# A new order for the softmax, state and transpose steps of a hybrid attention block

## The reference

```python
h = rmsnorm(x, norm_g); proj = h @ w_in
gk = jax.nn.log_sigmoid(gk_lr @ w_gk_up + b_gk) / 16
o_gla  = rmsnorm(gla_chunked(q, k, v, gk), gla_norm_g) * silu(gate_g)       # 4 heads, chunks of 64
o_pool = (multiscale_pool(u_p) @ pool_w) * pool_scale * silu(gate_p)
s = einsum('bthd,bmhd->bhtm', q_m, k_m) * 64 ** -0.5                        # 4 heads, 256 memory tokens
o_mem  = einsum('bhtm,bmhd->bthd', softmax(s), v_m) * silu(gate_m)
y = rmsnorm(x + concat(o_gla, o_pool, o_mem) @ w_out, final_g)
```

## Time and profile before

| | |
|---|---|
| Median of 3 runs | 1545.3 us (1544.16 to 1546.3) |
| The profiled execution: its time, its span | 1545.3 us, 1543.8 us |
| Mean granted TensorE clock | 0.973 |
| Busy share of TensorE, VectorE, ScalarE, GpSimd | 93%, 47%, 39%, 15% |
| One block of the loop | 87.8 us |

### The profile page before, as it was taken

How to read it: one execution, slowest core, us unless ns; L and a number is a source line. 1 busy time by engine, 2 the same in 40 slices (tenths; PEclk the granted TensorE clock), 3 DMA queues, 4 the chain that set the end, 5 groups by cost and what they waited for, 6 DMA issues and landing times.

```text
span 1543.8 us, 28261 instructions
## 1 busy us (share of the span) xinstructions
PE 1443.0 (93%) x11746; PEld 1046.2 (68%) x11746; DVE 724.0 (47%) x1221; ACT 608.1 (39%) x1101; POOL 236.4 (15%) x217
## 2 busy tenths in 40 slices
PE   3359699999999999999999999999999999999996
PEld 2238476776867677676867677686867767686762
DVE  2876625436172535527163544627163543616253
ACT  1344425344342534434252534434262534434241
POOL 1231201121110201121020202121020112112000
PEclk9669799999999999999999999999999999999998
DMA  8130100102010010102001010202001010201001
GB/s 337 65 136 1 42 2 28 54 0 82 0 69 12 27 54 10 71 0 82 0 36 46 27 54 0 82 0 82 0 27 54 21 61 0 82 0 46 10 28 68
DMA packets 15432, 69.32 MB, mean 45 GB/s; under 512 B 2352, under 2 KB 2480, under 8 KB 12848
## 3 DMA queue, kind: packets, MB, share of 16 engines
q1 hardware_dynamic: 15408, 68.98, 11.9%
HBM read 52.20 MB, written 16.78 MB: 45 GB/s over the span
## 4 chain that ended last, share of the span: by engine, by line
PE 90%; DVE 4%; ACT 2%; DMA 1%; issue 1%; POOL 1%; SPq 1%; DVEq 0%; ACTq 0%; POOLq 0%
PE bank L330 75%; PE bank L484 2%; PE bank L452 2%; PE bank L490 2%; PE bank L476 2%; PE bank L498 2%; DVE whl L852 1%; PE bank L541 1%; DVE wmx L816 1%; PE bank L463 1%; PE bank L388 1%; DMA whl<-in_pool_w 1%; PE bank L435 1%; PE bank L380 1%; POOL arena L1134 1%
## 5 line engine op out<-in xcount | busy, mean ns | idle before, releaser
L330 PE MATMUL bank<-arena,whl 128*128 128x256 f16 x6144 | 684.6, 274 | 2.6 <-DVE whl L852 2.6
L330 PEld LDWEIGHTS bank<-arena,whl 128*128 128x128 f16 x6144 | 602.3, 98 | 84.1 <-issue 6.5
L330 PE MATMUL bank<-arena 128*128 128x512 f16 x1536 | 344.1, 381 | 6.4 <-DVE arena L872 6.4
L330 PEld LDWEIGHTS bank<-arena 128*128 128x128 f16 x1536 | 147.8, 98 | 181.3 <-issue 15.4
L963 DVE SCALAR_TENSOR_TENSOR arena<-arena 64x256 f32<-64x256 f32 x60 | 25.2, 420 | 314.6 <-POOL arena L1191 313.2
L330 PE MATMUL bank<-whl,arena 128*128 128x512 f16 x768 | 168.3, 379 | 0.0
L686 ACT ACTIVATE arena<-bank,sca 128x512 f32<-128x512 f32 x64 | 43.9, 688 | 254.4 <-PE bank L330 253.3
L330 PEld LDWEIGHTS bank<-whl,arena 128*128 128x128 f16 x768 | 75.2, 99 | 86.9
L1143 POOL TENSOR_TENSOR arena<-arena 128x1024 f16<-128x1024 f32 x32 | 77.8, 2451 | 285.7 <-ACT arena L621 285.7
L1134 POOL TENSOR_TENSOR arena<-arena 128x1024 f32<-128x1024 f32 (+2 forms) x48 | 76.7, 1599 | 231.7 <-ACT arena L599 222.6
L1184 POOL TENSOR_TENSOR arena<-arena 128x542 f32<-128x542 f32 x16 | 17.4, 1090 | 606.1 <-ACT arena L693 598.3
(11 more groups left out here) (154 smaller groups left out, 1467.9 us busy)
## 6 DMA issues: line engine op xcount, KB each, us to landing
arena<-in_xt SPq DMA_DIRECT2D x16, 1024.0 KB, 5.2
arena<-in_x SPq DMA_DIRECT2D x32, 512.0 KB, 3.3
out<-arena SPq DMA_DIRECT2D x32, 512.0 KB, 2.6
arena<-in_w_in SPq DMA_DIRECT2D x8, 768.0 KB, 16.1
arena<-in_w_out SPq DMA_DIRECT2D x1, 4096.0 KB, 12.2
arena<-in_w_in SPq DMA_DIRECT2D x8, 392.0 KB, 16.2
arena<-in_w_mem SPq DMA_DIRECT2D x1, 2048.0 KB, 11.0
arena<-in_memt SPq DMA_DIRECT2D x1, 1024.0 KB, 6.6
```

The lines of the kernel that those rows point to most:

```text
L330: mm = nc.tensor.matmul(ap, lhs, rhs, start=k == 0 and n == 0, stop=(k, n) == last)
```

## The change

It changes the order of steps in the programs of TensorE, ScalarE and VectorE and nothing else. On TensorE the chunk states go ahead of scores 2 and 3, `quarter(1)` goes behind `turn_p(0, 6)`, and `turn_p(2, 6)` goes ahead of `quarter(2)` and the sum of squares. On ScalarE the table load goes ahead of `ket`, and `p_hi_of(3)` behind `norm_y`. On VectorE `p_norm(1)` goes ahead of `p_low(0)`, `state(0)` and `state(1)` go ahead of `mem_max(2)` and `(3)`, and `p_low(3)` goes behind `pt_copy(1, 7)`.

```diff
@@ TensorE @@
                 quarter(0)
+                states(0)
+                states(1).then_inc(pe_st, 1)
                 mem_scores(2)
                 mem_scores(3)
-                states(0)
-                states(1).then_inc(pe_st, 1)
-                quarter(1)
                 pe.wait_ge(sT_ok, 2 * i + 1)
                 turn_p(0, 6)
+                quarter(1)
                 pe.wait_ge(sT_ok, 2 * i + 2)
                 turn_p(1, 7)
+                pe.wait_ge(pt_out, 4 * i + 1)
+                turn_p(2, 6)
                 quarter(2)
                 if not last:
                     pe.wait_ge(p_exp, 4 * i + 4)
                     rms_sum(i + 1)
-                pe.wait_ge(pt_out, 4 * i + 1)
-                turn_p(2, 6)
                 pe.wait_ge(pt_out, 4 * i + 2)
                 turn_p(3, 7)
@@ ScalarE @@
                 silu(6, 3, 6)
+                nc.scalar.preload_act_table_set(EXP_LN)
                 act.wait_ge(pe_ket, i + 1)
...
                                      ACT.Copy).then_inc(ket_out, 1)
-                nc.scalar.preload_act_table_set(EXP_LN)
@@ ScalarE @@
                 p_hi_of(2)
-                p_hi_of(3)
                 if not first:
                     norm_y(i - 1, 0)
+                p_hi_of(3)
@@ VectorE @@
                 p_norm(0)
+                p_norm(1)
                 p_low(0)
-                p_norm(1)
                 p_low(1)
                 rows(0)
+                state(0)
+                state(1)
                 mem_max(2)
                 mem_max(3)
-                state(0)
-                state(1)
                 pt_copy(0, 6)
                 p_norm(2)
                 p_norm(3)
                 p_low(2)
-                p_low(3)
                 rows(1)
                 state(2)
                 pt_copy(1, 7)
+                p_low(3)
                 state(3)
                 pt_copy(2, 6)
```

## The result

The changed kernel takes 1582.7 us (median) against 1544.7 us before: 2.4% slower, ratio 1.0241 (95% interval 1.0221 to 1.0261), or 38.0 us. 1587.5 us were predicted, with a range of 1571 to 1607. Of the changed kernel's timed executions three took 1580.9 to 1582.8 us and one, in a slow state that no trace explains, 6496.0 us; the ratio leaves that one out.

What follows compares the result with a forecast made beforehand. TensorE, with no waits in loop blocks 1 to 14, was taken to bound the kernel. 14 x 2.70 = 37.8, plus 0.9, 0.2 and 3.3, made 42.2 us on 1545.3: 1587.5 us, range 1571 to 1607.

Steps and rivals of the forecast that it cites:

- What bounds it: Loop blocks 1 to 14: TensorE has no wait there, so a new order can only cost nothing or add waits.
- Edit 1: Table load ahead of ket on ScalarE: ket ends later, so TensorE's quarter(0) starts 0.85 us late in each block.
- The release: Time from ket's end to the start of the waiting quarter(0): taken as 0.1 us, bounds 0.05 to 0.15.
- Edit 2: States ahead of scores 2 and 3, reciprocals together, state(0) and (1) ahead of maxima: maxima 0.11 us later.
- Edit 3: turn_p(2) ahead of quarter(2), turn_p(0) ahead of quarter(1): TensorE waits another 1.85 us for p_low(2) in each loop block.
- the two waits: Waits for ket (0.85 us) and p_low(2) (1.85): 2.70 per loop block; a smaller first makes the second larger.
- Edit 4: p_hi(3) behind norm_y, p_low(3) behind pt_copy(1): turn_p(3) keeps 1.9 us of slack, so no cost.
- The ends: Block 15 0.9 us longer (bounds 0.85 and 2.70), block 0 about 0.2 us longer (bounds -1.7 and +1).
- Clock: TensorE's granted clock in the loop: two falls behind the new pauses, 3.3 us, between bounds of nothing and 23.4.
- B: Rival: the pauses make the clock fall in most blocks, 9 to 14 falls, 1599 to 1608 us; chance 0.25.
- Sum: Whole kernel: 37.8 us for the loop, plus 0.9, 0.2 and 3.3, is 42.2 us slower.

Runs made afterwards that it cites:

- undoing edit 1: The changed kernel with only the table load put back behind ket on ScalarE; 1581.2 us, ratio 1.0238.
- edit 4 undone: The changed kernel with p_hi(3) ahead of norm_y and p_low(3) behind p_low(2) again; 1581.3 us, ratio 1.0242.
- edit 3 alone: The kernel before with turn_p(0) moved ahead of quarter(1) and turn_p(2) ahead of quarter(2); 1579.3 us, ratio 1.0229.

## Why the prediction was right

- **What bounds it.** No wait in the loop before, so nothing to gain. All twelve variants agree: none is faster by more than can be measured, and each loss in the loop is a wait of TensorE, plus falls of its clock.
- **Edit 1, 0.85 us late**: measured 0.99. The release was mis-sized: the matmuls start 0.24 us behind ket's end (785.25 to 785.49), not 0.1, and outside the bounds of 0.05 to 0.15, which came from a release by VectorE. It has no effect on the sum, since the wait ahead of turn_p(2) shrinks by as much.
- **Edit 2, maxima 0.11 us later**: measured 0.07.
- **Edit 3, turn_p(2) bound to p_low(2), 2.70 us a block**: measured 2.67; the wait itself 1.51 of idle time. That the two waits share one end, and do not add, was the step that mattered, and undoing edit 1 showed it.
- **Edit 4 at nothing**, with quarter(2) as its cover: right for this kernel. The words "the cover is quarter(2)" were wrong as they stand: quarter(2) stands there in the kernel before too, and there edit 4 costs 0.75 us a block. What covers it is that the whole of TensorE is late, by 2.67 us in the changed kernel.
- **The ends.** Block 15's quarter(0) was 0.81 us late (1509.30 - 1507.61, against 1472.48 - 1471.60), as said, but the execution did not get longer by it. TensorE's wait for the last maximum of the mixture shrank from 2.4 to 1.1 us. There the store and the next fetch of rows set the pace, and the store is issued 21.34 us behind the first scores (1528.95 - 1507.61) in place of 21.89 (1493.49 - 1471.60). So the end is 0.5 us shorter and not 0.9 longer. That norm_y ahead of p_hi(3) brings this is argued from the order and not shown by a run of its own. Block 0 took 87.46 us in place of 87.92, where 0.2 us more was forecast.
- **Clock, 3.3 us for two falls**: measured none, in 14 blocks with pauses of 1.51 us. This is the larger part of the 4.8 us by which the forecast was too high. The two falls were chosen between bounds and not worked out, so that the clock held was in part luck. The mechanism is real, and B was nearer than its chance of 0.25 sounds: behind a pause half a microsecond longer the clock fell in 8 of 14 blocks.
- **Sum.** Forecast 42.2 us, of which 37.8 for the loop; measured 38.0, of which 37.4 to 37.6 for the loop. The two profiled executions differ by only 35.6 us: besides the loop's 37.6, the set-up was 1.1 us shorter, without a change to it, and blocks 0 and 15 each 0.5 us.

## What to carry to other kernels

Where the busiest engine has no wait, reordering can only add some; for each step that is moved earlier, ask when its input is ready, and follow that chain through the in-order queues of the other engines. Waits in series that hang on one late input don't add: undoing the first makes the second longer, so the price of an edit alone is not its price in the set, and an edit that is free in one order can cost in another (edit 4: nothing in the changed kernel, 0.75 us a block in the one before; the states ahead of the maxima: nothing before, 1.22 us a block in the changed one).

## What the runs showed of the hardware

The granted clock fell behind pauses shorter than the 3.8 us of the trace before. Over the 14 loop blocks of one profiled execution each:

| Pause ahead of turn_p(2), us | Blocks with a fall |
|---|---|
| 1.51 (changed kernel, and with edit 4 undone) | 0 |
| 1.77 (edit 3 alone) | 0 |
| 1.85 (edit 1 undone) | 0 |
| 2.0 (p_low(2) behind `state(2)`) | 8 |
| 2.45 (turn_p(2) alone) | 13 |
| 2.6 (p_low(2) behind `pt_copy(1, 7)`) | 6 |

Each fall held the clock at 0.50 for 3.4 us and cost 1.7 us. The Trainium skill ("TensorE: Matmul & The Clock Gate", section "A second HAM failure mode: psum-queue depth-cycling") warns of frequent small pauses; by the pauses of 2.0 us and more the traces agree, by those up to 1.85 us they do not.

The length of the pause alone does not explain the counts: one of 2.45 us had more falls than one of 2.6. The traces point to the moment of the pause as well. With turn_p(2) alone moved, the 13 falls of the loop and that of block 15 begin 92.2 us apart, each behind the last. A block with a fall lasts 92.1 to 92.2 us there, so the next pause comes as far behind the last fall as the one before did, and another fall follows. In the run with 2.6 us the falls of the loop begin 92.2, 184.3 or 276.5 us apart, one, two or three times the same distance, though its blocks last 91.6 to 91.7 us without a fall and 93.0 to 93.3 with one. With 2.0 us they begin 92.2 or 184.3 us apart. This is read from the traces; no run moves a pause in time alone. If it holds, the counts do not rank the pauses, and a 0 in the table names no length that is safe. The runs also differ in what stands ahead of the pause (two groups of transposes with turn_p(2) alone, one in the others), and none separates that from the moment.

The table load took 1.28 us and began 0.02 us behind the instruction ahead of it, before and after. From the end of ScalarE's ket to the start of the matmuls that waited for it went 0.24 us (785.25 to 785.49), from the end of VectorE's p_low(2) to the transposes 0.15 us (800.28 to 800.43).
